# Mixture-of-experts chunks of 32 rows in four column tiles instead of 64 rows in two

## The reference

```python
top_v, top_i = lax.top_k(logits, TOP_K)              # 4 of 32 experts per token
for e in range(N_EXPERTS):
    z = xt @ w_up[e] + b_up[e]                       # 1024 -> 2048
    gate = jnp.minimum(z[:, :D_EXPERT], SWIGLU_LIMIT)
    up = jnp.clip(z[:, D_EXPERT:], -SWIGLU_LIMIT, SWIGLU_LIMIT)
    act = (up + 1.0) * gate * jax.nn.sigmoid(SWIGLU_ALPHA * gate)
    out = out + gate_dense[:, e:e + 1] * (act @ w_down[e] + b_down[e])
```

## Time and profile before

| | |
|---|---|
| median of 3 runs | 1721.73 us (1720.87 to 1728.93) |
| profiled execution | 1725.74 us, its span 1723.9 us |
| mean granted TensorE clock | 0.911 |
| PE busy | 1509.4 us, 88% |
| up pieces L1264, down pieces L1286 | 491.8 us and 256.0 us busy |
| weight DMAs | 384 of 1 MB |
| part of the span from the first chunk's gather to the end of PE's work | 674.9 to 1678.4 us |

### The profile page before, as it was taken

The page is one execution under the profiler, slowest core; times in us unless marked ns, Lnnn a source line. Parts: engine busy times, 40 slices in busy tenths (PEclk is TensorE's granted clock), DMA queues, the critical chain, the costliest instruction groups (busy, mean ns, idle before and its releaser), DMA issues.

```text
span 1723.9 us, 21845 instructions
## 1 busy us (share of the span) xinstructions
PE 1509.4 (88%) x8284; PEld 669.8 (39%) x8285; DVE 379.5 (22%) x803; ACT 291.9 (17%) x541; POOL 84.8 (5%) x122
## 2 busy tenths in 40 slices
PE   5998989869977955999999998999999899998980
PEld 5544556458854523333333232333332232232220
DVE  6010011346723253111010101010111010010106
ACT  5000013543511010111111101111111111011110
POOL 1000003100000000000000000000000000000002
PEclk9999987978996975999999999999999998999995
DMA  9746764681154632996999999899999999999954
GB/s 277 247 149 230 267 244 117 202 295 42 50 161 137 257 142 100 395 416 267 404 418 417 419 417 419 353 416 418 419 416 419 417 418 419 416 419 417 419 224 158
DMA packets 139315, 527.56 MB, mean 306 GB/s; under 512 B 11554, under 2 KB 40634, under 8 KB 104259
## 3 DMA queue, kind: packets, MB, share of 16 engines
q1 hardware_dynamic: 128482, 482.81, 71.3%
q0 software_dynamic: 10784, 44.07, 7.5%
HBM read 499.85 MB, written 31.15 MB: 308 GB/s over the span
## 4 chain that ended last, share of the span: by engine, by line
PE 58%; DMA 15%; SPq 15%; DVE 8%; issue 3%; ACT 2%; POOL 0%; POOLq 0%; DVEq 0%; ACTq 0%
PE bank L1264 18%; SPq L627 12%; DMA arena<-in_b_up 10%; PE bank L1286 7%; PE bank L1116 4%; PE bank L736 3%; PE bank L941 3%; DMA arena<-in_w_in 3%; PE bank L942 3%; PE bank L1258 2%; PE bank L1189 2%; SPq L632 2%; DMA arena<-in_cache_cmp,arena 1%; PE bank L1177 1%; PE bank L1275 1%
## 5 line engine op out<-in xcount | busy, mean ns | idle before, releaser
L1264 PE MATMUL bank<-arena 128*64 128x512 f32 x2176 | 491.8, 610 | 0.0
L1264 PEld LDWEIGHTS bank<-arena 128*64 128x64 f32 x2176 | 155.3, 140 | 338.3 <-issue 338.3
L1286 PE MATMUL bank<-arena 128*64 128x512 f32 x1088 | 256.0, 625 | 0.0
L2057 DVE TENSOR_SCALAR arena<-bank 128x512 f32<-128x512 f32 x34 | 23.5, 692 | 836.9 <-PE bank L1264 836.9
L1286 PEld LDWEIGHTS bank<-arena 128*64 128x64 f32 x1088 | 77.8, 143 | 154.8 <-issue 154.8
L1572 ACT ACTIVATE arena<-arena 128x512 f32<-128x512 f32 x34 | 21.4, 629 | 524.4 <-DVE arena L2057 524.4
L1234 PE MATMUL bank<-arena 128*64 128x512 f32 (+1 forms) x420 | 103.1, 609 | 8.0 <-DVE arena L2047 8.0
L2134 POOL DMA_DIRECT2D slots<-arena x68 | 36.0, 529 | 1294.3 <-ACT arena L1579 1292.1
L1116 PE MATMUL bank<-arena 128*128 128x288 f32 x256 | 77.2, 453 | 12.9 <-DMA arena<-in_w_in 9.9
L1258 PE MATMUL bank<-arena 1*64 1x512 f32 x272 | 41.6, 683 | 36.8 <-DMA arena<-in_b_up 35.2
L941 PE MATMUL bank<-arena 128*128 128x512 f32 (+1 forms) x112 | 58.4, 604 | 7.3 <-DMA arena<-in_w_in 5.7
(11 more groups left out here) (387 smaller groups left out, 1324.8 us busy)
## 6 DMA issues: line engine op xcount, KB each, us to landing
arena<-in_w_up SPq DMA_DIRECT2D x256, 1024.0 KB, 19.3
arena<-in_w_down SPq DMA_DIRECT2D x128, 1024.0 KB, 22.6
arena<-in_w_ada SPq DMA_DIRECT2D x12, 2048.0 KB, 10.8
slots<-arena POOLq DMA_DIRECT2D x2, 6400.0 KB, 37.0
arena<-in_w_in SPq DMA_DIRECT2D x6, 2048.0 KB, 12.7
slots<-arena POOLq DMA_DIRECT2D x68, 128.0 KB, 5.5
arena<-in_w_in SPq DMA_DIRECT2D x16, 512.0 KB, 3.9
arena<-in_w_out SPq DMA_DIRECT2D x1, 4096.0 KB, 17.4
```

Of the source, the lines that this page charges most:

```text
L1264: last = mm(banks[part][SLOT * s:SLOT * s + SLOT, :], xcT[:, q], ring[pos][:, D * part + 512 * s:D * part + 512 * s + 512], start=False, s ...
L1286: last = mm(banks[4][SLOT * s:SLOT * s + SLOT, :], lhs, ring[pos][:, D * v + 512 * s:D * v + 512 * s + 512], start=False, stop=f == 7)
```

## The change

SLOT becomes 32 and a constant Q = 256 is added. Each output half of 1024 columns is made by four matmuls of 256 columns in four column tiles of PE (32 columns each) instead of two matmuls of 512. The tiles that DVE and ACT handle become 128x256. PE's first up piece opens the accumulation and the bias matmuls (eight of 256 columns) come behind it. SP issues an expert's bias rows ahead of its first piece. A chunk's result is stored by four DMAs of 32 x 256. The `slots` table has 68 x 32 = 2176 rows instead of 50 x 64 = 3200. With these inputs there are 52 chunks: 15 experts have one, 15 have two, expert 3 has three and expert 13 has four. The count of chunks per expert is made by a comparison with multiples of 32 and a sum.

```diff
-SLOT = 64
+SLOT = 32
+Q = D // 4
...
                 for q in range(4 if two_back is None else 0, 12):
                     before, part = (two_back, q + 8) if q < 4 else (back, q - 4)
                     sp.wait_ge(S("piece_used"), before * 12 + (part + 1))
+                    if q == 0:
+                        load_bias(e, j)
                     load_piece(e, j, q)
-                    if q == 3:
-                        load_bias(e, j)
...
-                        for r in range(4):
-                            mm(banks[r // 2][SLOT * (r % 2):SLOT * (r % 2) + SLOT, :], one(r), row(r)[:, 0:512], start=True, stop=False)
                         for q in range(8):
                             pos, use = (12 * j + q) % 16, (12 * j + q) // 16
                             pe.wait_ge(S(f"ld_piece{pos}"), grp * 48 + 16 * use + 16)
                             for part in range(2):
-                                for s in range(2):
-                                    last = mm(banks[part][SLOT * s:SLOT * s + SLOT, :], xcT[:, q],
-                                              ring[pos][:, D * part + 512 * s:D * part + 512 * s + 512], start=False, stop=q == 7)
+                                for s in range(4):
+                                    last = mm(banks[part][SLOT * s:SLOT * s + SLOT, 0:Q], xcT[:, q],
+                                              ring[pos][:, D * part + Q * s:D * part + Q * s + Q], start=q == 0, stop=q == 7)
                             last.then_inc(S("piece_used"), 1)
+                            if q == 0:
+                                for half in range(2):
+                                    for r in range(4):
+                                        s = 2 * (r % 2) + half
+                                        mm(banks[r // 2][SLOT * s:SLOT * s + SLOT, 0:Q], one(r), row(r)[:, Q * half:Q * half + Q],
+                                           start=False, stop=False)
                         pe.wait_ge(S("oneslot"), c + 2)
                         dispatch()
+                        pe.wait_ge(S("yc"), c)
                         pe.wait_ge(S("act"), c + 1)
-                        for k in range(4):
+                        for k in range(2):
                             last = nc.tensor.transpose(banks[3][:, P * k:P * k + P], ac[:, P * k:P * k + P], ident)
                         last.then_inc(S("aT_ps"), 1)
-                        pe.wait_ge(S("yc"), c)
...
-                for s in range(2):
-                    pool.dma_start(slots[bass.ds(c * SLOT, SLOT), 512 * s:512 * s + 512], yc[SLOT * s:SLOT * s + SLOT]
+                for s in range(4):
+                    pool.dma_start(slots[bass.ds(c * SLOT, SLOT), Q * s:Q * s + Q], yc[SLOT * s:SLOT * s + SLOT]
```

More of the change, by code:

```diff
@@ L472, in build @@
         h2T = mT
-        gt, up, sg, ac = (view(gate_at + 512 * i, 512) for i in range(4))
+        gt, up, sg, ac = (view(gate_at + Q * i, Q) for i in range(4))
         in_chunk = [view(gate_at + 12 * NCHUNK * i, 12 * NCHUNK, 12, NCHUNK) for i in range(2)]
-        aT, yc, xr = (view(x_at + 3 * D + 512 * i, 512) for i in range(3))
-        xcT = view(mod_rows_at + 3 * D, 512, KD, SLOT)
+        aT, yc, xr = (view(x_at + 3 * D + Q * i, Q) for i in range(3))
+        xcT = view(mod_rows_at + 3 * D, KD * SLOT, KD, SLOT)
         oneslot = view(mod_rows_at + 3 * D + 512, 3 * SLOT, 3, SLOT)
@@ L1262, in _ @@
                             for part in range(2):
-                                for s in range(2):
-                                    last = mm(banks[part][SLOT * s:SLOT * s + SLOT, :], xcT[:, q],
-                                              ring[pos][:, D * part + 512 * s:D * part + 512 * s + 512], start=False, stop=q == 7)
+                                for s in range(4):
+                                    last = mm(banks[part][SLOT * s:SLOT * s + SLOT, 0:Q], xcT[:, q],
+                                              ring[pos][:, D * part + Q * s:D * part + Q * s + Q], start=q == 0, stop=q == 7)
                             last.then_inc(S("piece_used"), 1)
+                            if q == 0:
[4 more added lines that the diff above has]
+                                           start=False, stop=False)
                         pe.wait_ge(S("oneslot"), c + 2)
                         dispatch()
+                        pe.wait_ge(S("yc"), c)
                         pe.wait_ge(S("act"), c + 1)
-                        for k in range(4):
+                        for k in range(2):
                             last = nc.tensor.transpose(banks[3][:, P * k:P * k + P], ac[:, P * k:P * k + P], ident)
                         last.then_inc(S("aT_ps"), 1)
-                        pe.wait_ge(S("yc"), c)
-                        for s in range(2):
-                            mm(banks[4][SLOT * s:SLOT * s + SLOT, :], one(s), row(s)[:, 512:1024], start=True, stop=False)
+                        for half in range(2):
+                            for r in range(2):
+                                s = 2 * r + half
+                                mm(banks[4][SLOT * s:SLOT * s + SLOT, 0:Q], one(r), row(r)[:, 512 + Q * half:512 + Q * half + Q],
+                                   start=True, stop=False)
                         pe.wait_ge(S("xr"), c + 2)
@@ L1283, in _ @@
                                 f = 2 * (q - 8) + v
[L1284 to L1287, removed]
+                                lhs = aT[:, P * (f % 2) + SLOT * (f // 2):P * (f % 2) + SLOT * (f // 2) + SLOT]
+                                for s in range(4):
+                                    last = mm(banks[4][SLOT * s:SLOT * s + SLOT, 0:Q], lhs,
+                                              ring[pos][:, D * v + Q * s:D * v + Q * s + Q], start=False, stop=f == 7)
                             last.then_inc(S("piece_used"), 1)
@@ L2020, in _ @@
             after(dve, "cnt_ps")
[L2021 to L2026, removed]
+            link(dve, "dve", V.tensor_copy(idxf[0:E, 0:1], banks[3][0:E, 0:1]))
+            link(dve, "dve", V.tensor_scalar(roww[0:E, 0:JMAX - 1], C("iota")[0:E, 1:JMAX], float(SLOT), idxf[0:E, 0:1], ALU.mult, ALU.is_lt))
+            link(dve, "dve", V.tensor_reduce(idxf[0:E, 1:2], roww[0:E, 0:JMAX - 1], AX, ALU.add))
+            V.tensor_scalar(nchT[0:E], idxf[0:E, 1:2].broadcast_to([E, P]), 1.0, None, ALU.add).then_inc(S("nch"), 1)
             after(dve, "base_ps")
```

26 lines of the change are left out of this document (13 added, 13 removed).

## The result

The changed kernel takes 1742.07 us, median of 4 runs (1740.25 to 1744.49). Beside it the kernel before took 1722.51, median of 4 runs (1720.87 to 1728.93). The ratio is 1.0097, with a 95% interval of 1.0068 to 1.0126: slower by about 1%, which is more than the 0.5% that can be told from no change. 1749 was forecast, 1715 to 1767 as the range. The profiled execution took 1744.49 us with a span of 1742.7; before it was 1725.74 and 1723.9, so 18.8 us are to be found in the traces.

A forecast was written before the change was run, and what follows sets the result against it. The prediction took the arrival of 384 MB of expert weights by DMA (416 to 420 GB/s) as the bound. From 1721.7 us, terms 1 to 5 added 1 and term 6 added 26, giving 1749 us; range 1715 to 1767.

The forecast's parts named there:

- term 6: PE's loop code: grows from 1095 to 2027 instructions, is refetched each later pass, 63 fetches loading DMA engines: +26 us.
- Term 1: Start of the weight stream: shorter work before the first held-back piece, partly offset by larger slot tables: -4.0 us.
- term 4: Zero fill of slots: smaller first fill brings the second some 8 us forward onto gate pieces; -9 or +4, taken as 0.
- Term 2: DMA gaps at experts 3 and 13: idle time grows from 18.9 to 31.1 us, +12.2 us.
- (n-2) x Y - 7.6: Idle DMA time in us at an expert with n chunks: none for two, 6.7 at expert 3, 21.0 at expert 13.
- Y: PE's time for one new 32-row chunk: estimated 14.2, taken as 14.3 us, bounds 13.5 to 28.
- Term 3: Tail after the last weights: PE ends about 1.3 us after the last piece instead of 9; -7 us in sum.
- Term 5: Result stores: 52 x 128 KB instead of 34 x 256 KB; fewer bytes -3, more rows +7, taken as 0.
- the code still fits: Rival on PE's loop code: nothing is refetched, terms 1 to 5 alone, 1723 us, no difference; chance 27%.
- The faster one: Rival at the zero fill: the gate piece lands in time, PE's 9.3 us wait goes, code fits, 1714 us; chance 11%.
- The half clock in dense chunks: Rival at experts 3 and 13: half clock stays, 28 us per chunk, gaps 68 instead of 31 us, 1760 us; chance 7%.
- The tiles overlap beside full DMA traffic: Opposite of a rival: PE's four column tiles do not overlap, about 27 us per chunk, about 2120 us; chance 3%.

The follow-up runs named there:

- merged: Changed kernel with gate and up made by one 512-column matmul instead of two of 256, loop body 1452 instead of 2028 instructions: 1726.33 us, ratio 1.0005.
- written-out form: Changed kernel with the loop over the eight expert groups written out in line, nothing else changed: 1719.36 us, ratio 0.9983.
- the late fill: Second zero fill held behind four gate-piece uses: kernel before with bias first, 1705.07 us (0.9869); changed kernel with group loop in line, 1709.62 us (0.9929).

## Why the prediction was right, and where it was not

The sign was right, and so was the reading that PE's code would be outgrown and fetched again in each pass. The sum was 7 us high. But 26 of its 27 us came from term 6, and the mechanism by which that term was priced was wrong; that it came out near is luck.

- **Term 1, start, and term 4, zero fill.** Predicted -4.0 and 0, measured -2.3 together. The second fill came 8.5 us earlier, as forecast ("some 8"), onto the gate pieces, as forecast. Of its two outcomes neither held whole: PE's wait of 9.29 became 5.84 and 1.70 at two pieces, and SP's queue was held up. The run with the old size of the fill shows no price of it (372.0 against 371.4), so 0 was right; the start then gave 2 us where 4 were forecast.
- **Term 2, gaps.** That the gaps come from the chunks beyond the second is shown by their absence with at most two chunks. The rule (n-2) x Y - 7.6 gives 6.7 and 21.0 us; the gaps were 8.9 and 23.7. The forecast added 1.7 to each for a half clock, which did not come (granted 1.00 in both gaps, 1.05 us for a piece); so 8.4 and 22.7 were near for a reason that failed, and some 2 us of each gap are open. Y was 14.5 for 14.3. The rule also takes PE to be close behind the pieces: expert 4 with two chunks had a gap of 6.8 us after a stall. The difference was +14.3 for +12.2, as the gaps before are 18.3 by the packets and not 18.9, and those after are 1.5 us longer.
- **Term 3, tail.** -5.5 for -7: PE ends 2.0 us after the last weights, not 1.3, and the end behind it grew by 1.4.
- **Term 5, stores.** 0 predicted, and the pace gained 0.26 us an expert, some 7 us. The merged and the written-out form have about the same gaps and no stall, and their stretch from the first held-back piece to PE's end (992.6 and 991.3) is near that of before (990.2) although their gaps cost 14 more: the shorter tail gives 7 of it back and the pace the other 7. Fewer bytes account for most of the pace, and the -3 of the forecast was too small: 34 x 256 KB less 52 x 128 KB are 2.1 MB, 5 us at 417 GB/s as an estimate. Rows of 1 KB, put at +7, show no cost. No run tried the stores by themselves.
- **Term 6, PE's code.** That it is outgrown is shown: 109 fetches for "some 100", ten or so in each pass, and none again at 1452 instructions. The price failed in its step. It was built from the load of 63 fetches on a DMA engine, 38 us at most, 26 taken; that load costs nothing that shows, as the written-out form and the equal pace with and without fetches (30.97 and 30.96) show. The step "PE's own stall at each jump back is hidden: a one-chunk expert leaves it 31.2 - 14.3 us" is the one that was wrong. It holds for five of the seven jumps: heads 20, 24 and 28 have one chunk, and at 8 and 12 PE was at most 1.2 us behind the pieces. It does not hold at heads 4 and 16, which are two-chunk experts behind the dense experts 3 and 13. The sentence speaks of one-chunk experts only, and PE is some 29 and 17 us late there before the stall begins. The stalls of about 7 us cost 16 to 20 us in all. So 26 was near, but for another reason than its own.

Terms 5 and 6 together were 26 in the forecast and some 11 in the traces; with 2 more in the gaps and 3 more at both ends the sum comes to about 18 instead of 27.

The Trainium skill, "Runtime: NRT & Kernel Launch", section "Instruction fetch mechanics", says what happens here: a taken branch to code outside the window forces a fetch before execution can go on, while straight code is fetched ahead. The traces agree on both halves (7.08 us at the jump, 0.39 written out), and with its 2048 instructions as far as 1452 stay and 2189 do not; 2028 lies just below and does not stay either, which fits only with its blocks of 256, as the prediction had it, and was not tested by itself. The window of two pages of which the section speaks does not fit: 1452 instructions are six or seven blocks, and they stay.

Of the rivals, "the code still fits" was built and gave what it said, 1726 for 1723. The faster one did not come: PE still waited 7.5 us for gate pieces. The half clock in dense chunks did not come: 1.00 in both gaps. The tiles overlap beside full DMA traffic, 14.5 us a chunk.

Not settled: some 2 us in each of the two gaps, some 2 of the 7 us gained in pace, and why the late fill gained more than PE's wait.

## What to carry to other kernels

Count the instructions of a loop body on each engine before splitting its matmuls finer, since code that is outgrown costs a stall at each jump back, and look where these jumps fall: a stall is free while the stream still has buffers to fill, and costs about its full length where the engine is already late and the next buffer comes free only a whole chunk later. Smaller tiles help an engine that is not the bound only by its latency at the end, and they multiply the time of whoever has three or more of them while no buffer is handed back. A bulk fill that nobody needs soon can be held back behind the loads that somebody waits for; here that gained 0.5% with chunks of 32 rows and 1.1% with chunks of 64.

## What the runs showed of the hardware

- A jump back to code that is no longer held stopped PE for 6.80 to 7.52 us beside a weight stream of 408 GB/s (4.10 to 5.37 in the kernel before with eight experts in the loop), and PE was at the lower clock for 10 us behind it (a piece took 1.94 us instead of 1.05). A body of 1452 instructions stays, bodies of 2028 and 2189 are fetched anew in each pass, 10 to 11 blocks of 16.4 KB each time.
- Four fp32 matmuls of 512 columns in four column tiles of 32 take the time of eight of 256 (1.05 to 1.07 us), with half the instructions.
- A fill of 4352 KB on another queue ahead of SP's loads came with longer issues on SP itself: 5.58 us instead of 1.12 and 8.49 instead of 1.63. With the fill at its old size, when it was issued at 343.61 beside them, they took 1.05 and 1.95.
- In the steady part the granted clock was 0.87 in the changed kernel (PE busy 226 of 300 us, waits for pieces), 0.93 in the kernel before (277, waits for `b_up`) and 0.98 in that with the bias first (274). So the busy time alone does not order the clocks, and as the stream sets the pace there, none of them shows in the time of an expert (30.97, 31.23, 31.22 us).
